# Token norms summed into 128 partitions, the first two tiles of two projections run in quarters, and key norms summed per head in 32 partitions

## What is computed

```python
# first block
h = rms(x, norm_mix_pre) * (1 + sc_m) + sh_m
r, k, v = einsum(x_rkv, w_rkv)                 # three 2048 x 2048 projections
kk = heads(k * k_k)                            # 32 heads of 64 channels
kk = kk * rsqrt(maximum(sum(kk * kk, axis=-1), 1e-24))
...                                            # chunked scan, group norm, gate
y = ... @ w_o
x = x + g_m * rms(y, norm_mix_post)            # first residual
h = rms(x, norm_ffn_pre) * (1 + sc_f) + sh_f
u = causal_dwconv(h @ ffn_w_in); f = (silu(gate) * val) @ ffn_w_out
x = x + g_f * rms(f, norm_ffn_post)            # second residual
# second block
z = rms_norm(x, norm_gain) @ w_in              # q, k, v, gates, convolution
...                                            # attention, convolution, @ w_out
x = x + sigmoid(rms_norm(x) @ w_gate + b) * rms_norm(p @ w_ple_proj)
```

## Time and profile before

| | us |
|---|---|
| median of 3 runs | 1961.63 (1959.37 to 1962.23) |
| profiled execution | 1961.79 |
| its span, first to last instruction | 1960.0 |
| PE busy in it | 1915.0 |
| DVE, ACT, POOL busy | 1434.8, 906.0, 121.9 |
| mean granted clock of TensorE | 0.994 of full |

### The profile page before, as it was taken

How to read it: one execution, slowest core, us unless ns; L and a number is a source line. 1 busy time by engine, 2 the same in 40 slices (tenths; PEclk the granted TensorE clock), 3 DMA queues, 4 the chain that set the end, 5 groups by cost and what they waited for, 6 DMA issues and landing times.

```text
span 1960.0 us, 32673 instructions
## 1 busy us (share of the span) xinstructions
PE 1915.0 (98%) x12802; PEld 1661.8 (85%) x12802; DVE 1434.8 (73%) x2025; ACT 906.0 (46%) x1476; POOL 121.9 (6%) x126
## 2 busy tenths in 40 slices
PE   7999999998999989999999999999999999999998
PEld 5888888888888878888888888888888888888887
DVE  7997969324869988888877776444477967777876
ACT  3346321142335455555555555444455436645554
POOL 0000002000023200000000000000020000002200
PEclk9999999999999999999999999999999999999999
DMA  9996424554429746666555556555535544445553
GB/s 393 421 420 231 150 104 155 215 225 186 187 97 418 309 176 235 239 250 252 199 193 191 191 188 225 191 189 188 191 150 198 181 173 172 172 172 215 193 179 123
DMA packets 58936, 418.34 MB, mean 213 GB/s; under 512 B 6673, under 2 KB 7057, under 8 KB 12561
## 3 DMA queue, kind: packets, MB, share of 16 engines
q1 hardware_dynamic: 52210, 366.59, 50.9%
q0 software_dynamic: 6336, 46.14, 6.1%
q10 hardware_dynamic: 288, 4.19, 0.5%
HBM read 410.60 MB, written 6.29 MB: 213 GB/s over the span
## 4 chain that ended last, share of the span: by engine, by line
PE 87%; DVE 7%; DMA 3%; issue 2%; ACT 1%; POOL 1%; SPq 0%; DVEq 0%; ACTq 0%; POOLq 0%
PE ps L716 44%; PE ps L719 22%; PE ps L693 10%; PE ps L836 2%; DMA bk<-in_ada 2%; DVE ar L1921 1%; DMA zb<-in_ada 1%; PE ps L831 1%; PE ps L1107 1%; PE ps L852 1%; PE ps L1030 1%; POOL h L600 1%; DVE mixb L1973 0%; DVE bk L1728 0%; PE ps L923 0%
## 5 line engine op out<-in xcount | busy, mean ns | idle before, releaser
L716 PE MATMUL ps<-x_pair,whi 128*128 128x512 f32 x2464 | 790.3, 397 | 5.3 <-issue 2.8
L1750 DVE TENSOR_TENSOR wlo<-ring,whi 128x1024 fp32r<-128x1024 f32 x468 | 551.1, 1213 | 102.7 <-ACT whi L1269 98.8
L719 PEld LDWEIGHTS ps<-x_pair,wlo 128*128 128x128 f32 x2464 | 463.1, 188 | 95.4
L719 PE MATMUL ps<-x_pair,wlo 128*128 128x256 f32 x2464 | 510.7, 278 | 0.0
L1269 ACT ACTIVATE whi<-ring 128x1024 fp32r<-128x1024 f32 x468 | 462.5, 1031 | 97.4 <-PE ps L719 94.8
L716 PEld LDWEIGHTS ps<-x_pair,whi 128*128 128x128 f32 x2464 | 386.4, 188 | 23.2 <-issue 9.2
L1276 ACT ACTIVATE px<-ps 128x256 f32<-128x256 f32 x202 | 77.5, 384 | 443.0 <-PE ps L719 443.0
L716 PE MATMUL ps<-hid_pair,whi 128*128 128x512 f32 x688 | 216.8, 395 | 0.0
L719 PEld LDWEIGHTS ps<-hid_pair,wlo 128*128 128x128 f32 x688 | 129.3, 188 | 29.9
L693 PE MATMUL ps<-mixb,ring 128*128 128x256 f32 x640 | 142.2, 384 | 1.8 <-issue 1.8
L693 PEld LDWEIGHTS ps<-mixb,ring 128*128 128x128 f32 x640 | 122.6, 192 | 19.4 <-issue 2.2
(11 more groups left out here) (309 smaller groups left out, 2323.8 us busy)
## 6 DMA issues: line engine op xcount, KB each, us to landing
ring<-in_fi SPq DMA_DIRECT2D x86, 1024.0 KB, 4.8
ring<-in_zin SPq DMA_DIRECT2D x52, 1024.0 KB, 4.8
ring<-in_fo SPq DMA_DIRECT2D x32, 1024.0 KB, 4.9
ring<-in_ada SPq DMA_DIRECT2D x26, 1024.0 KB, 6.4
bk<-in_ada SPq DMA_DIRECT2D x22, 1024.0 KB, 18.0
ring<-in_wr SPq DMA_DIRECT2D x16, 1024.0 KB, 4.8
ring<-in_wv SPq DMA_DIRECT2D x16, 1024.0 KB, 4.8
ring<-in_wo SPq DMA_DIRECT2D x16, 1024.0 KB, 9.3
```

The lines of the kernel that those rows point to most:

```text
L716: mm(ps[:, bank, 0:2 * S], whi[:, slot, j * P:(j + 1) * P], x2(k0 + j), start=first and j == 0, stop=False, skip_group_check=True)
L719: m = mm(ps[:, bank, 0:S], wlo[:, slot, j * P:(j + 1) * P], x2(k0 + j)[:, 0, :], start=False, stop=last and j == n - 1, skip_group_check=True)
L1750: V.tensor_tensor(wlo[:, hf % WB, 0:m], ring[:, u % RING, 1024 * x:1024 * x + m], whi[:, hf % WB, 0:m].bitcast(F32), ALU.subtract).then_in ...
```

## The change

Three things are changed together.

1. The mean squares of tokens in the two residuals are summed with the squares as weights and a column of ones as the moving operand (`token_sums`), which gives one number per token in two columns of 128 partitions. Root and inverse work on these (128x2), and two matmuls with the identity spread the result over the partitions (`token_spread`) into a PSUM bank, which DVE multiplies from. The last tile's square comes before its scaled copy.
2. The first two tiles of `fi` and of `zk` run in quarters, both tiles for each quarter of x (`two_by_pieces`), where before only the first tile was cut, in halves. The weights' halves of the second tile are prepared earlier, one modulation product moves from `wo` to `fi`, DVE's order in the second residual goes quarter by quarter, and POOL's additions of `zsq` wait for the end of the residual additions. L1117 now stands behind the pieces.
3. The squared keys are summed with a 0/1 matrix of 32 columns into 32 partitions, one for each head. Root, clamp and inverse work on 32x256. 32 matmuls (`key_spread`) spread it to the channels in PSUM, from where DVE multiplies. PE runs five tiles of r ahead of the grams instead of eight.

The core of it on PE and POOL:

```diff
                 pool.dma_start(ada_w(j % 4), t["ada"][66 + j]).then_inc(ld_adw[j % 4], 16)
                 if j >= 4:
...
                 pool.wait_ge(rms_sq[4], q + 1)
+                pool.wait_ge(x_done, 2 * NT)
                 if q > 1:
                     pool.wait_ge(zsq_sum, q - 1)
                 nc.gpsimd.tensor_tensor(zsq[:, 0, :], zsq[:, 0, :], zsq[:, q, :], ALU.add).then_inc(zsq_sum, 1)
...
+            def token_sums(src, first, last):
+
+                for tt in range(TT):
+                    m = mm(ps[:, 7, tt:tt + 1], src[:, tt * P:(tt + 1) * P], const("ones"), start=first and tt == 0,
+                           stop=last and tt == 1, skip_group_check=True)
+                return m
+
+            def token_spread(k):
+
+                pe.wait_ge(rms_rec, k + 1)
+                for tt in range(TT):
+                    m = mm(tok_bc(k)[:, tt * P:(tt + 1) * P], tok_rs[:, tt:tt + 1].to_broadcast([P, P]), ident,
+                           start=True, stop=True)
+                m.then_inc(rms_bc, 1)
...
+                for k in range(2):
+                    bank_free(TILE[name] + k)
+                for p in range(4):
+                    pe.wait_ge(x_lo, rdy + p)
+                    for k in range(2):
+                        m = split_tiles(half_in(name, 2 * k + p // 2), p % 2 * 4 + 4, x2, p // 2 * 8, (TILE[name] + k) % BANKS,
+                                        p < 2, p >= 2, RUN[name], p % 2 * 4)
+                        if p % 2 and (k == 0 or p == 3):
+                            m.then_inc(pe_step, 1 if k == 0 else 2)
+                    if between:
+                        between(p)
...
-            for q in range(8):
-                pe.wait_ge(k_sq, 2 * q + 2)
-                if q >= 4:
-                    pe.wait_ge(hs_root, q - 3)
-                for e in range(2):
-                    m = mm(ps[:, 4 + q % 4, e * S:(e + 1) * S], const("blk"), ar_i[:, 2 * q + e, 1, :], start=True, stop=True)
-                m.then_inc(hs_sum, 1)
+            for i in range(NT):
+                pe.wait_ge(k_sq, i + 1)
+                o = NH - 2 - 2 * i
+                m = mm(ps[0:NH, 4, 0:S], const("sel")[:, o:o + NH], ar_i[:, i, 1, :], start=i == 0, stop=i == NT - 1)
+            m.then_inc(hs_sum, 1)
+
+            def key_spread(half):
+
+                pe.wait_ge(hs_rec, 1)
+                for i in range(8 * half, 8 * half + 8):
+                    if half and i % 2 == 0:
+                        pe.wait_ge(hs_used, i // 2 - 3)
+                    for e in range(2):
+                        m = mm(ps[HD * e:HD * e + HD, 4 + i // 2 % 4, i % 2 * S:(i % 2 + 1) * S],
+                               ident[0:NH, 2 * i + e:2 * i + e + 1].to_broadcast([NH, HD]), sq_sum[0:NH, :],
+                               start=True, stop=True)
+                    if i % 2:
+                        m.then_inc(key_bc, 1)
...
-            for k in range(8):
+            project("r", mixa, 0)
+            key_spread(0)
+            project("r", mixa, 1)
+            project("r", mixa, 2)
+            key_spread(1)
+            for k in range(3, R_AHEAD):
                 project("r", mixa, k)
...
-            keep_clock(5, 6)
-            rms(1, None, NT - 1, (TILE["wo"] + NT, mixb[:, NT - 1, :]))
-            keep_clock(10, 6)
+            pe.wait_ge(sq_acc, NT - 1)
+            token_sums(sq_sum, True, False)
+            keep_clock(1, 6)
+            pe.wait_ge(tile_free, TILE["wo"] + NT)
+            token_sums(mixb[:, NT - 1, :], False, True).then_inc(rms_sum, 1)
+            keep_clock(1, 6)
+            token_spread(1)
+            keep_clock(7, 6)
             rms(2, mixb)
-            keep_clock(22, 6)
-
-            project_split("fi", tiles_of(x_pair), 2 * FT, x_rdy=((x_lo, 2), (x_lo, 4)))
+            keep_clock(15, 6)
+
+            two_by_pieces("fi", tiles_of(x_pair), 1)
+            project_split("fi", tiles_of(x_pair), 2 * FT, first=2)
...
-            rms(3, None, 2 * NT - 1, (TILE["fo"] + NT, fsq[:, (NT - 1) % 2, :]))
-            for k in range(1, 5):
+            pe.wait_ge(sq_acc, 2 * NT - 1)
+            token_sums(sq_sum, True, False)
+            pe.wait_ge(tile_free, TILE["fo"] + NT)
+            token_sums(fsq[:, (NT - 1) % 2, :], False, True).then_inc(rms_sum, 1)
+            p_tile(1, 0)
+            token_spread(3)
+            p_tile(1, 1).then_inc(e_mm, 1)
+            for k in range(2, 5):
                 p_pair(k)
-            keep_clock(8, (TILE["zk"] + 3) % BANKS)
...
-            project_split("zk", x2, 12, after_zk, ((x_lo, 6), (x_lo, 8)), two_pairs)
...
+            def p_between(p):
+                if p == 0:
+                    p_pair(5)
+                elif p == 1:
+                    p_pair(6)
+                    p_pair(7)
+
+            two_by_pieces("zk", x2, 5, p_between)
+            pe.wait_ge(zsq_sum, 3)
+            for i in range(4):
+                m = mm(ps[:, 7, 0:S], const("ones").to_broadcast([P, P]), zsq[:, 0, i * S:(i + 1) * S],
+                       start=i == 0, stop=i == 3)
+            m.then_inc(rms_sum, 1)
+            project_split("zk", x2, 12, after_zk, first=2)
```

On ACT and DVE:

```diff
+            def token_root(k):
+                act.wait_ge(rms_sum, k + 1)
+                act.wait_ge(rms_rec, k)
+                A(tok_rt, ps[:, 7, 0:2], ACT.Sqrt, scale=1.0 / D, bias=const("eps")[:, 0:1]).then_inc(rms_root, 1)
...
+                    if last:
+                        hi_part(after, 1, halves=(0,))
...
-                ops(n - 1, join_in(name, n - 1)).then_inc(tile_free, 1)
+                squared, rest = last_ops(n - 1, join_in(name, n - 1))
+                squared().then_inc(tile_free, 1)
+                rest()
...
-            for q in range(8):
-                act.wait_ge(hs_sum, q + 1)
-                A(ar_i[:, 2 * q:2 * q + 2, 1, :], ps[:, 4 + q % 4, :].rearrange("p (i s) -> p i s", s=S), ACT.Sqrt
-                  ).then_inc(hs_root, 1)
+            act.wait_ge(hs_sum, 1)
+            A(sq_sum[0:NH, :], ps[0:NH, 4, 0:S], ACT.Sqrt).then_inc(hs_root, 1)
...
             act.wait_ge(gates_rdy, 1)
-            evac_split("wo", NT, raw_and_square(cum, gates=0), "fi")
-            root(1)
+            evac_split("wo", NT, raw_and_square(cum, gates=0), wo_last, "fi")
+            token_root(1)
+            hi_part("fi", 1, halves=(1,))
...
-                    if k + 1 < 2 * FT:
+                    if k == 0 and it is None:
+                        pass
+                    elif k + 1 < 2 * FT:
                         hi_part("fi", k + 1, it)
...
             p_out(0)
-            hi_part("zk", 1)
+            hi_part("zk", 1, halves=(1,))
             for q in range(4):
                 p_out(q + 1)
                 act.wait_ge(x_done, NT + 4 * q + 4)
                 for i in range(4 * q, 4 * q + 4):
                     scaled_hi(i, "n2")
-            for q in range(4):
-                A(zsq[:, q, :], xr[:, 4 * q:4 * q + 4, :].rearrange("p i s -> p (i s)"), ACT.Square).then_inc(rms_sq[4], 1)
-                if q < 2:
-                    p_out(5 + q)
+                if q:
+                    residual_square(q - 1)
+            p_out(5)
+            residual_square(3)
+            p_out(6)
+            p_out(7)
...
                             lo_part(after, 0)
+                            lo_part(after, 1, halves=(0,))
...
+            def token_rec(k):
+
+                dve.wait_ge(rms_root, k + 1)
+                V.reciprocal(tok_rs, tok_rt).then_inc(rms_rec, 1)
+                dve.wait_ge(rms_bc, 1 if k == 1 else 2)
...
-                        V.tensor_tensor(yq, yq, rms_rs.unsqueeze(1).to_broadcast([P, w, S]), ALU.mult).then_inc(sprd, 1)
+                        V.tensor_tensor(yq, yq, tok_bc(k).unsqueeze(1).to_broadcast([P, w, S]), ALU.mult).then_inc(sprd, 1)
...
-                    if q >= 2 and k == 3:
+                    if k == 3:
                         yield
...
+            dve.wait_ge(hs_root, 1)
+            own(V.tensor_scalar(sq_sum[0:NH, :], sq_sum[0:NH, :], 1e-12, None, ALU.max))
+            V.reciprocal(sq_sum[0:NH, :], sq_sum[0:NH, :]).then_inc(hs_rec, 1)
             for b in range(8):
 
-                dve.wait_ge(hs_root, b + 1)
-                root, d = (ar_i[:, 2 * b:2 * b + 2, a, :] for a in (1, 0))
-                own(V.tensor_scalar(root, root, 1e-12, None, ALU.max))
-                own(V.reciprocal(root, root))
-                V.tensor_tensor(d, d, root, ALU.mult).then_inc(hs_used, 1)
+                dve.wait_ge(key_bc, b + 1)
+                d = ar_i[:, 2 * b:2 * b + 2, 0, :]
+                V.tensor_tensor(d, d, ps[:, 4 + b % 4, :].rearrange("p (i s) -> p i s", s=S), ALU.mult).then_inc(hs_used, 1)
...
-                dve.wait_ge(ld_adw[k % 4], 16 * (k // 4 + 1))
-                dot_into(66 + k, ada_w(k % 4))
+                if k < WO_DOTS:
+                    dve.wait_ge(ld_adw[k % 4], 16 * (k // 4 + 1))
+                    dot_into(66 + k, ada_w(k % 4))
+                else:
```

(58 more changed lines are left out.)

101 lines of the change are left out of this document (50 added, 51 removed).

## The result

The changed kernel takes 1970.85 us (median of 20 runs, 1962.28 to 1974.37), the kernel before 1962.31 us (20 runs, 1958.26 to 1967.69). The ratio is 1.0034, 95% interval 1.0025 to 1.0043: some 6.7 us slower, by more than the 0.2% that a measurement tells. The profiled execution took 1972.98 us, is 11.2 us longer in its span than that of before, and lies among the longer of its 20. The forecast was 1965.1 us (+3.3 on 1961.79), its range ended at 1969.5. The ratio applied to the same 1961.79 gives 1968.5: the direction is the one forecast, the size twice it. "No change" had 0.56 of the chances and "slower", which came, 0.29.

The account below looks back on a forecast made before the run. PE was taken as the bound, busy 1915.0 of 1960.0 us, so other engines' savings count only where PE waits. Keys +4.5, first residual -3.7 and second +2.5 make +3.3 on 1961.79: 1965.1 us, range 1956.5 to 1969.5.

Parts of the forecast that it names:

- Keys, +4.5 us: At the keys: new spread matmuls lengthen PE's work while DVE's savings were mostly hidden; net +4.5 us.
- The rival that the spreads don't overlap: At the keys: paired spreads run one after the other, +10.7 us there, total 1971.3 us; chance 0.08.
- Net: 7.7 - 3.2 = +4.5 us: At the keys: 16 spread pairs cost PE 7.7 us, minus its 3.2 us wait for DVE that goes.
- First residual, -3.7 us: From `wo` to the third `fi` tile: shorter chain and quarters, less a new weights wait; -4.0 + 0.3 = -3.7 us.
- Chain: First residual, from the end of `wo` to DVE's first product: 2.2 us shorter (1.7 to 2.7).
- the 0.3 for the fifth tile: First residual: a chain with a modulation product makes the fifth tile some 0.3 us late.
- Second residual, +2.5 us: POOL's additions and DVE's rests alternate, PE waits 5.6 us; +0.5 us plus 2 us of half clock.
- DVE coming first: Second residual: DVE's rests go ahead of POOL's additions, -3.45 in place of +2.5, total 1959.1 us; chance 0.27.
- both side by side: Second residual: POOL's additions and DVE's rests interleave at no price, -5.15 us, total 1957.4 us; chance 0.12.
- Forecast -1.2 for the residuals: The two residuals' terms together: -3.7 us in the first and +2.5 us in the second.
- 0.03 of the chances: Whole kernel: the chance of 0.03 set aside for what the prediction did not see.

Follow-up runs that it names:

- the pads: The kernel before with 32 (`before_gpad`) or 64 (`before_gpad64`) one-column matmuls, read by nobody, directly ahead of the grams; ratios 1.0021 and 0.9996.
- before_gpad: The kernel before with 32 one-column matmuls, read by nobody, directly ahead of the grams; ratio to the kernel before 1.0021 (1.0010 to 1.0033).
- pool_late: The changed kernel with POOL's three additions of the last norm held back until DVE's last rest; ratio to the kernel before 1.0000 (0.9987 to 1.0013).
- before_gpad64: The kernel before with 64 one-column matmuls, read by nobody, directly ahead of the grams; ratio to the kernel before 0.9996 (0.9982 to 1.0010).
- third_early: The changed kernel with the first half of the third `fi` tile's weights split ahead of the first tile's copy; ratio to the kernel before 1.0021.

## Where the prediction held, and where it was short

Its working stood in kind at every place that it named, and it missed one that it did not. The sign came out right because the keys' term did; that the ratio still fell within the range is luck, as the range was made for the clock and for POOL, and not for the term that was missing.

- **Keys, +4.5 us.** Held: 0.45 us a pair instead of 0.48, the grams at 233.09 where 233 stood. After the second transposes (260.12 with seven r tiles done, 276.44 with ten before; three tiles are 20.8 us) the change is 4.5 us behind. The rival that the spreads don't overlap, 1971.3 us, has the measured total and is refuted by that row: a total that agrees is no evidence for a mechanism.
- **The step that was short** is the end of that same term: "Net: 7.7 - 3.2 = +4.5 us". It priced the 32 matmuls where they stand and took everything behind them as only shifted. They also move the bounds of PE's code blocks by half a block, and one bound then falls among matmuls of 17 ns each. Shown by the pads: 32 cost 4.1 us (1.0 to 3.3 thousandths), 64 nothing (-1.8 to +1.0). Part of the 4.1 is the longer wait (1.82 to 3.85 us in the traces). The clock behind it goes with the bounds' place (0.95 against 1.00 over 35 us, which is 3.5 us at half clock); how much of the rest is that is not measured. Some may lie elsewhere: in the second residual `before_gpad` has the same wait of 2.79 us as the kernel before, but with half clock behind it, and takes 35.20 us instead of 33.84.
- **First residual, -3.7 us.** Chain 2.08 us shorter (forecast 2.2), `fi` after 23.85 us (23.7), the wait 2.53 us (2.6), third tile -3.7 (-4.0; the 0.3 for the fifth tile did not come). Left out was the half clock behind the wait, 2.9 us long (729.7 to 732.6), 1.5 us. At `fo`'s end 1.6 us are left of the gain.
- **Second residual, +2.5 us.** Held in kind: rests and additions by turns, PE waits 4.34 us (5.6), clock at half behind it; the third tile starts 35.50 us after `fo`'s end instead of 33.84, +1.7. DVE coming first and both side by side are refuted by the 9.59 us. That the contention would eat the whole gain of this part was in the numbers, and `pool_late` shows it: 2.65 us are gained there without it.
- **Sum.** Forecast -1.2 for the residuals, measured -1.6 (0.9992). With 4.5 for the keys and 4.1 for the blocks this makes 7.0 us; the ratio says 6.7. The two measured ones are good to some 2 us each, so that the sum agrees so well is partly luck. The term that was missing is larger than any that was worked out but one, and it had 0.03 of the chances. The other 2.7 us that the profiled execution lost between the inverse and `wo` go with a half clock of some 10.2 us in the group norm against 6.8; `before_gpad64` has 10.2 there too and is no slower by its ratio, so no run here ascribes it to the change.

## What to carry to other kernels

Where a profile shows waits that end with "issue" among short matmuls, count PE's records between them: if they are multiples of one length, every edit ahead of them can have a second price that depends on its number of instructions, not on its work. Compare two versions of such a kernel with a pad that gives both the same bounds, or the difference is partly that of their code's place. And work that an edit lets start at a common point (here DVE's rests and POOL's additions) is to be put in order by hand: the one on the path first.

## What was unexpected of the hardware

- The waits with "issue" in the inverse fit code blocks of 128 f32 matmul records: they stood 256 (changed), 383 (before) and 255 (`before_gpad`) records apart, moved by 64 records with 32 added matmuls and back with 64. Among the small matmuls the wait was 3.1 to 4.3 us (the longest in `pool_late`), in the v tile 0.7 to 1.9.
- PE resumed 2.0 to 2.8 us behind the instruction packet that moved amid the weights: packet between 441.5 and 442.0 and resumption at 444.09 before, 439.5 to 440.0 and 441.96 in `before_gpad`, 444.5 to 445.0 and 447.32 in the changed kernel.
- Behind a wait of 2.53 us the clock was at half (0.50 from 730 to 732), and in `third_early`, where PE ran through, it stayed at 1.00 up to 730. But behind the same wait of 2.8 us in the second residual it stayed at 1.00 in the kernel before and fell to 0.50 in `before_gpad`; what tells the two apart no row shows.
